# Down projection of a two-layer decoder trunk: seven block products for eight of its eleven K pairs, in two passes of 512 channels

## The chip, the cores and the metric

The kernel runs on one core of a Trainium2 chip. The metric is the device time of one execution in microseconds (us); smaller is better. Engines are named as in the profile: PE is TensorE (PEld its weight loads), DVE VectorE, ACT ScalarE, POOL GpSimd, SP SyncE, which issues most transfers.

## What is computed

Two layers, each with four mixers side by side, an output projection and a SwiGLU block. The change is in the last but two lines:

```python
x = x + rms_norm(y, attn_post_g[l])
h = rms_norm(x, ffn_pre_g[l])
f = jax.nn.silu(jnp.einsum('bsd,df->bsf', h, w_gate[l])) * jnp.einsum('bsd,df->bsf', h, w_up[l])
f = jnp.einsum('bsf,fd->bsd', f, w_down[l])
x = x + rms_norm(f, ffn_post_g[l])
```

Here s is 512 tokens, d is 1024, and the hidden width f is 2816, which is 22 blocks of 128. All is float32; the result of one layer is the x of the next.

## The kernel before

Each float32 operand of a large product is held as two float16 parts, hi and lo, and every product is three matmuls (hi hi, hi lo, lo hi; `split3`, line 582). Weights come from memory as "slots" of 128 x 2048 float32 (1 MB), in four parts of 512 columns, into the buffer `raw`, which holds two slots and four more parts. For each part ACT copies raw to the hi half of a place in the float16 buffer `ring` (`split_hi_chunk`, recorded at line 925), and DVE writes the lo half (`split_lo_part`, line 1413). `ring` has 32 "quads" of 1024 float16 each: an ordinary slot takes four, a fast one seven. ACT and DVE are strictly in program order; a split waits on them until the quads it overwrites are free, and SP loads the next part of raw when DVE has read the old one.

PE walks a list `UNITS` of (slot, token tiles). Per layer: ten slots of the input projection, four of the output projection, 22 of gate/up (one for each hidden block f) and eleven of the down projection (each has two K blocks of 128, the "pair"). Between the matmuls of a unit PE places small products (attention, transposes) at numbered ticks; the table `AT` says which tick, and `h_T` (eight transposes of a normalised tile) is entered there as `pre_T` and `fpre_T`.

**Gate/up.** The hidden blocks 5 to 21 (`FAST`) are already made by seven products of 256 columns instead of eight (`seven_products`, line 661): 84 matmuls per block. Their weight sums are made by two DVE additions (lines 1389, 1392) and two adding transfers from POOL. Within a unit PE waits for ACT and DVE four times: `p1_copied` (ACT copies the first product), `u_sb` and `v_sb` (ACT copies of sums, `u_copy`, `v_copy`) and `c12_ps` (a DVE addition, `c12_add`, line 1450). Beside the unit of block f, `main_steps` of ACT and DVE also finish the hidden block f-1 (`silu` line 1100, `hidden` line 1780, `hidden_hi`, `hidden_lo` line 1788) and split the weights that follow, in four chunks between these steps. At the end of gate/up two slots of the down projection are split beside one unit, because they need only four quads each.

**Down.** For each slot and tile PE makes 12 matmuls of 512 columns, 24 for a pair and 512 channels over all four tiles. The four results of the tiles lie in the eight PSUM banks (`pair(t)`). The first seven slots run over all tiles; of the last four (`DN_TAIL`) all are done for tile 0, then tile 1, 2 and 3, so that the norm of a finished tile runs beside the next ones: per tile ACT squares (`square_y`), DVE makes the root (seven instructions, `rstd`) and adds to x (`norm_y`, lines 1492 and 1495), ACT squares x, DVE makes the root and `norm_x` (line 1527), PE transposes (`h_T`), ACT and DVE write `hT` (`h_hi_of`, `h_lo_of` line 1535). In the last layer `norm_out` (lines 1508, 1511) takes the place of `norm_y` and the tile is stored.

```python
split_lo(*REST[l])
norm_y("fpost", l, 0)
norm_x("pre", l + 1, 0)
norm_y("fpost", l, 1)
```

`REST[l]` are the slots whose split follows after gate/up: in layer 0 the last down slots 44 to 46 and the first four of layer 1 (47 to 50).

## Time and profile before

| | us |
|---|---|
| median of 3 runs (1065.86 to 1069.61) | 1068.95 |
| the profiled execution, its own time | 1068.87 |
| its span in the trace | 1067.1 |
| PE busy | 1044.1 (98%) |
| DVE busy | 759.4 (71%) |
| ACT busy | 498.6 (47%) |
| share of the chain that ended last: PE / DVE / ACT | 92% / 3% / 2% |

Times of the trace count from the start of the span. A busy PE is not a PE at its peak, since matmuls overlap and their ends are modelled; the distance between the starts of matmuls is what counts.

### The profile page before, as it was taken

The page shows a single profiled execution, that of the slowest core. Times are in us where ns is not written, and L with a number is a line of the kernel's source. Part 1 is how long each engine was busy: PE and PEld are TensorE (multiplying, and loading weights), DVE is VectorE, ACT ScalarE, POOL GpSimd, SP SyncE. Part 2 cuts the span into 40 slices and gives each one's busy share as a digit, 9 for nine tenths or more (in the row PEclk, how much of TensorE's full clock was granted, in tenths as well). Part 3 has the DMA queues.
Part 4 walks back from the last instruction along what each step waited for, and adds up shares of the span by engine and source line. Part 5 has one row for each costly group of instructions (what it writes and reads, how often), then busy time and mean ns, then how long its engine had stood idle before and what let it go on. Part 6 is the DMA issues. An engine that isn't in the chain of part 4 may idle for free.

```text
span 1067.1 us, 19775 instructions
## 1 busy us (share of the span) xinstructions
PE 1044.1 (98%) x7894; PEld 776.7 (73%) x7894; DVE 759.4 (71%) x1571; ACT 498.6 (47%) x928; POOL 65.2 (6%) x86
## 2 busy tenths in 40 slices
PE   7999999999999999999999999999999999999997
PEld 5988895597888887444488888747878888864443
DVE  6999988987777877222679888898867777661014
...
DMA packets 72876, 136.59 MB, mean 128 GB/s; under 512 B 8657, under 2 KB 8913, under 8 KB 72657
## 3 DMA queue, kind: packets, MB, share of 16 engines
...
## 4 chain that ended last, share of the span: by engine, by line
PE 92%; DVE 3%; ACT 2%; issue 1%; DMA 1%; SPq 0%; ACTq 0%; DVEq 0%
PE ps L589 56%; PE ps L696 28%; PE ps L593 3%; PE ps L855 1%; PE ps L839 1%; DVE ring L1413 1%; ACT ring L925 1%; DMA xs<-x_dram 1%; PE ps L774 1%; PE ps L759 0%; DVE E L1527 0%; ACT gbc L925 0%; PE ps L816 0%; PE ps L777 0%; DVE hT L1535 0%
## 5 line engine op out<-in xcount | busy, mean ns | idle before, releaser
L1413 DVE SCALAR_TENSOR_TENSOR ring<-raw,ring 128x512 f16<-128x512 f32 (+1 forms) x368 | 293.4, 834 | 142.7 <-ACT ring L925 142.7
L925 ACT ACTIVATE ring<-raw 128x512 f16<-128x512 f32 (+1 forms) x368 | 252.0, 741 | 139.9 <-PE ps L589 76.7
L589 PE MATMUL ps<-ring,U 128*128 128x512 f16 x1440 | 313.4, 379 | 0.0
L589 PEld LDWEIGHTS ps<-ring,U 128*128 128x128 f16 x1440 | 140.8, 98 | 166.7 <-issue 0.3
L589 PE MATMUL ps<-hT,ring 128*128 128x256 f16 (+1 forms) x1632 | 195.2, 279 | 0.0
L589 PEld LDWEIGHTS ps<-hT,ring 128*128 128x128 f16 x1632 | 159.3, 98 | 28.9
L696 PE MATMUL ps<-E,ring 128*128 128x256 f16 x1224 | 146.7, 274 | 5.7 <-ACT ps L925 5.7
L696 PE MATMUL ps<-hT,ring 128*128 128x256 f16 x1224 | 146.1, 273 | 0.0
L589 PE MATMUL ps<-ring,hT 128*128 128x256 f16 x1152 | 134.8, 275 | 0.7 <-DVE hT L1535 0.7
L696 PEld LDWEIGHTS ps<-E,ring 128*128 128x128 f16 x1224 | 118.2, 98 | 22.9 <-ACT ps L925 7.4
L696 PEld LDWEIGHTS ps<-hT,ring 128*128 128x128 f16 x1224 | 120.2, 98 | 14.4
L589 PEld LDWEIGHTS ps<-ring,hT 128*128 128x128 f16 x1152 | 113.0, 99 | 15.8 <-issue 1.1
L1575 DVE SCALAR_TENSOR_TENSOR E<-E,par 128x256 f32<-128x256 f32 x240 | 102.1, 481 | 0.2
L566 POOL DMA_DIRECT2D raw<-weights_dram x34 | 29.8, 876 | 810.1 <-DMA raw<-weights_dram 810.1
L1100 ACT ACTIVATE R<-ps 128x512 f32<-128x512 f32 (+1 forms) x52 | 27.5, 528 | 92.4 <-PE ps L696 72.7
L1463 DVE TENSOR_SCALAR small<-small 128x1 f32<-128x1 f32 x31 | 4.6, 150 | 85.8 <-ACT E L935 77.2
L935 ACT ACTIVATE E<-ps 128x1024 bf16<-128x1024 f32 x15 | 15.3, 1019 | 90.6 <-PE ps L589 90.6
L696 PE MATMUL ps<-Z,ring 128*128 128x256 f16 x408 | 50.1, 273 | 0.0
L925 ACT ACTIVATE U<-ps 128x256 f32<-128x256 f32 (+3 forms) x56 | 30.2, 565 | 42.1 <-PE ps L593 15.3
L696 PEld LDWEIGHTS ps<-Z,ring 128*128 128x128 f16 x408 | 39.9, 98 | 4.6
L1780 DVE SCALAR_TENSOR_TENSOR R<-ps,R 128x512 f32<-128x512 f32 (+1 forms) x52 | 31.4, 604 | 5.8 <-ACT R L1100 5.1
L925 ACT ACTIVATE gbc<-ps 128x128 f32<-128x128 f32 (+3 forms) x32 | 13.9, 434 | 45.5 <-PE ps L855 36.2
...
## 6 DMA issues: line engine op xcount, KB each, us to landing
raw<-weights_dram SPq DMA_DIRECT2D x402, 256.0 KB, 3.5
raw<-weights_dram POOLq DMA_DIRECT2D x68, 256.0 KB, 6.1
...
U<-weights_dram SPq DMA_DIRECT2D x8, 256.0 KB, 7.7
out_dram<-xs SPq DMA_DIRECT2D x8, 256.0 KB, 2.0
...
bd<-pool_w_dram SPq DMA_DIRECT2D x8, 16.0 KB, 9.5
```

The costliest lines, as they stand in the source:

```text
L566: nc.gpsimd.dma_start(raw[:, x1, :], weights[PARTS * n, :, :], accum_op=ALU.add).then_inc(x1_sum[i % 2], 16)
L589: ins = mm(dst, st, mv_, start=first and i == 0, stop=last and i == 2, **kw)
L593: return nc.tensor.transpose(dst, src, ident)
L696: ins = mm(bank[b][:, 0:HALF], quad(n, q, pw)[:, cols], a[pa][:, k, :], start=first and k == 0 and j == 0, stop=last and k == KT // 2 - 1 ...
L774: last = mm(o[:, h, :], sm[:, h, :], rv[:, t, HD * h:HD * (h + 1)], start=h == 0, stop=t == 0 and h == NH - 1, skip_group_check=True)
L839: mm(bank[b][:, 0:P * (t + 1)], mqT[r, t % 2, h // 2, :], mkT[r, h // 2, 0:P * (t + 1)], start=False, stop=True, skip_group_check=True).th ...
L925: return A(dst, src, ACT.Copy, scale=scale)
L935: A(sink[:, :], pair(t), ACT.Square, scale=UNSCALE * DM ** -0.5, accum_out=ssq[:, t:t + 1]).then_inc(y_sq, 1)
L1100: A(like_gu(f, sil[:, n % 2, 0:P * len(tiles)]), gu_tiles(f, tiles)[0], ACT.Silu, scale=UNSCALE).then_inc(sil_done, 1)
L1413: V.scalar_tensor_tensor(out=at[1], in0=src, scalar=W_SCALE, in1=at[0], op0=ALU.mult, op1=ALU.subtract).then_inc(lo_split, 1)
L1575: ins = V.scalar_tensor_tensor(out=cacc[:, c, :], in0=src, scalar=w, in1=cacc[:, c, :], op0=ALU.mult, op1=ALU.add)
L1780: V.scalar_tensor_tensor(out=like_gu(f, fbuf[:, n % 2, 0:w]), in0=gu_tiles(f, tiles)[1], scalar=UNSCALE * A_SCALE * (-1.0 if f in FAST els ...
```

## The change

The pairs 2 to 9 of hidden blocks (blocks 4 to 19, `DN_FAST`) are multiplied as 2 x 2 blocks with seven products instead of eight: K is halved into the two blocks of a pair, tokens into halves of 256, and channels into quarters of 256. The channels are taken in two passes g of 512, so an item is (g, pair); it has 42 matmuls of 256 columns (`dn_seven`). The pairs 0, 1 and 10 (`PLAIN`) stay as they were; pair 10 follows the seven-product items of each pass, and pairs 0 and 1 are left for the end, tile by tile.

- The four sums of the hidden activations of a pair are made in gate/up, beside the unit after the pair's odd block: three DVE instructions (`fS_sums`), two ACT copies (`fS_hi`), two DVE instructions (`fS_lo`).
- The weight sums of an item are made by three DVE instructions (`dn_weight_sums`) before its split, which has 768 and 1024 columns instead of 512 and 512.
- After a pass the seven running sums in PSUM are combined: two ACT copies (`q11_copy`), six DVE instructions (`q_sums`); in pass 0 four more that add the pair-10 result (`y0_sums`). The combined sums lie in SBUF, and each finished tile gets them by one more DVE addition (`y_sum`) before its norm.
- Nine of the 32 quads now hold the activation sums of six pairs during gate/up and down (two pairs' lie in `Z` and `E`), so gate/up and down have 23. Only one slot is split beside a gate/up unit.
- ACT makes `p1_copy` after the first chunk of the split instead of the second.
- The transposes of tiles 0 and 1 for the next layer move: tile 0 to nine ticks before the end, tile 1 from layer 0 to tick 4 of layer 1, tiles 2 and 3 to ticks 26 and 52.
- The tail of the down projection has 30 matmuls of 512 columns for each tile (before: 48).

```diff
--- before.py
+++ after.py
-DN_TAIL = 4
 FAST = tuple(range(GU_HEAD + 1, FT))
+DN_FAST = tuple(range(2, 10))
+PLAIN = tuple(p for p in range(N_DN) if p not in DN_FAST)
+COVER = PLAIN[-1]
+ITEMS = [(0, p) for p in DN_FAST] + [(0, COVER)] + [(1, p) for p in DN_FAST] + [(1, COVER)]
+ITEMS += [(g, p) for p in PLAIN[:-1] for g in range(2)]
...
-UNITS += [(DN0, (t,)) for t in (2, 3, 0, 1)]
-UNITS += [(DN0 + c, (t,)) for c in range(1, N_DN - DN_TAIL) for t in TILES]
-UNITS += [(DN0 + c, (t,)) for t in TILES for c in range(N_DN - DN_TAIL, N_DN)]
+COVER_TILES = (2, 3, 0, 1)
+TAIL0 = 2 * len(DN_FAST) + 1
+WORK = {}
+
+
+def add_dn_unit(tiles, items):
+    WORK[len(UNITS)] = items
+    UNITS.append((DN0 + items[0] // 2, tiles))
+
+
+for k in range(TAIL0):
+    if ITEMS[k][1] == COVER:
+        for t in COVER_TILES:
+            add_dn_unit((t,), (k,))
+    else:
+        add_dn_unit(TILES, (k,))
+for t in TILES:
+    add_dn_unit((t,), (TAIL0,))
+    for k in range(TAIL0 + 1, len(ITEMS), 2):
+        add_dn_unit((t,), (k + 1, k))
...
+GU_RING = 23
...
+    if slot >= DN0:
+        size = (sum(HALF_QUADS[n]) + 1) // 2
+        top = top if top + size <= GU_RING else 0
+        places = list(range(top, top + size))
...
-        ("fpre_T", 0): 372, ("fpre_T", 1): 374, ("fpre_T", 2): 415, ("fpre_T", 3): 438, ("pre_T", 0): 955,
-        ("pre_T", 1): 965,
+        ("fpre_T", 0): 372, ("fpre_T", 1): 374, ("fpre_T", 2): 415, ("fpre_T", 3): 438, ("pre_T", 0): TICKS - 9,
...
-        ("pre_T", 2): 0, ("pre_T", 3): 31, ("moba_T", 0): 65, ("moba_T", 1): 82, ("moba_stage", 0): 106,
+        ("pre_T", 1): 4, ("pre_T", 2): 26, ("pre_T", 3): 52, ("moba_T", 0): 65, ("moba_T", 1): 82, ("moba_stage", 0): 106,
...
+                products = (
+                    (3, s1, [PAIR[3]], [(q_sb, q0 + 6)]),
+                    (4, s3, [PAIR[2]], [(q_sb, q0 + 3)]),
+                    (6, a22, [PAIR[2] + 1, PAIR[3] + 1], y_free[2:4]),
+                    (0, a11, [PAIR[0]], [(q11_sb, 2 * (2 * l + g) + 2)]),
+                    (5, s2, [PAIR[1]], [(q_sb, q0 + 2)]),
+                    (2, a12, [PAIR[0] + 1, PAIR[1] + 1], y_free[0:2]),
+                    (1, s4, [PAIR[0] + 1, PAIR[1] + 1], None))
+                for i, (blk, a, banks, free) in enumerate(products):
+                    if i:
+                        between(i)
+                    if first and free:
+                        for b, f_ in zip(banks, free):
+                            take(b, *f_)
+                    for t in range(2):
+                        if len(banks) == 1:
+                            dst, fresh = bank[banks[0]][:, HALF * t:HALF * (t + 1)], t == 0
+                        else:
+                            dst, fresh = bank[banks[t]][:, half(int(blk == 1))], blk != 1
+                        for c, (pw, pa) in enumerate(((0, 0), (1, 0), (0, 1))):
+                            ins = mm(dst, a[pa][:, tok(t)], dn_blocks(n, j, pw, blk, blk + 1),
+                                     start=first and fresh and c == 0, stop=last_ and c == 2, skip_group_check=True)
+                return ins
...
+            def fS_hi(l, p):
+
+                act.wait_ge(s_sum, 3 * fS_no(l, p))
+                copy(fS_w[p][:, 0, :], f_sum[:, 0:3 * HALF]).then_inc(s_hi, 1)
+                copy(fT[:, 0, 2 * p, half(1)], f_sum[:, 3 * HALF:4 * HALF]).then_inc(s_hi, 1)
...
-                    split_hi_chunks(new, 0, 2)
+                    split_hi_chunks(new, 0, 1)
                     if f in FAST:
                         p1_copy(l, f)
-                    split_hi_chunks(new, 2, 3)
+                    split_hi_chunks(new, 1, 3)
                     hidden_hi(l, *HIDDEN[i - 1])
                     if f in FAST:
                         u_copy(l, f)
+                    fp = HIDDEN[i - 1][0]
+                    if fp % 2 and in_seven(fp):
+                        fS_hi(l, fp // 2)
                     split_hi_chunks(new, 3, 4)
                     if f in FAST:
...
+                V.tensor_tensor(dn_sum(j)[:, 0:2 * HALF].rearrange("p (c t) -> p c t", c=2),
+                                three[:, 0:2 * HALF].rearrange("p (c t) -> p c t", c=2),
+                                b12.unsqueeze(1).to_broadcast([P, 2, HALF]), ALU.add).then_inc(x_sum, 1)
+                dve.wait_ge(x_sum, at + 1)
+                V.tensor_tensor(x[2], x[0], b22, ALU.add).then_inc(x_sum, 1)
+                dve.wait_ge(x_sum, at + 2)
+                V.tensor_tensor(x[3], x[2], b21, ALU.add).then_inc(x_sum, 1)
...
+                V.tensor_tensor(f_sum[:, 0:2 * HALF].rearrange("p (c t) -> p c t", c=2),
+                                f_all[:, HALF:3 * HALF].rearrange("p (c t) -> p c t", c=2),
+                                f_all[:, 3 * HALF:4 * HALF].unsqueeze(1).to_broadcast([P, 2, HALF]),
+                                ALU.subtract).then_inc(s_sum, 1)
+                dve.wait_ge(s_sum, i + 1)
+                V.scalar_tensor_tensor(out=f_sum[:, 2 * HALF:3 * HALF], in0=f_sum[:, 0:HALF], scalar=-1.0,
+                                       in1=f_all[:, 2 * HALF:3 * HALF], op0=ALU.mult,
+                                       op1=ALU.subtract).then_inc(s_sum, 1)
+                dve.wait_ge(s_sum, i + 2)
+                V.tensor_tensor(f_sum[:, 3 * HALF:4 * HALF], f_sum[:, 2 * HALF:3 * HALF], f_all[:, 0:HALF],
+                                ALU.add).then_inc(s_sum, 1)
...
+            def fS_lo(l, p):
+
+                dve.wait_ge(s_hi, 2 * fS_no(l, p))
+                V.tensor_tensor(fS_w[p][:, 1, :], f_sum[:, 0:3 * HALF], fS_w[p][:, 0, :],
+                                ALU.subtract).then_inc(s_lo, 1)
+                V.tensor_tensor(fT[:, 1, 2 * p, half(1)], f_sum[:, 3 * HALF:4 * HALF], fT[:, 0, 2 * p, half(1)],
+                                ALU.subtract).then_inc(s_lo, 1)
...
+            def q_sums(l, g):
...
+                for t in range(2):
+                    V.tensor_tensor(yq[2 + t][:, 512 + HALF:DM], p6[:, half(t)], yq[t][:, 512:512 + HALF],
+                                    ALU.add).then_inc(q_sb, 1)
+                dve.wait_ge(q_sb, i + 2)
+                V.tensor_tensor(yq23[:, :, 512:512 + HALF], p7[:, :].rearrange("p (t c) -> p t c", t=2),
+                                yq23[:, :, 512 + HALF:DM], ALU.add).then_inc(q_sb, 1)
+                for t in range(2):
+                    V.scalar_tensor_tensor(out=yq[t][:, 512 + HALF:DM], in0=p5[:, half(t)], scalar=-1.0,
+                                           in1=yq[2 + t][:, 512 + HALF:DM], op0=ALU.mult,
+                                           op1=ALU.subtract).then_inc(q_sb, 1)
+                dve.wait_ge(q_sb, i + 5)
+                V.scalar_tensor_tensor(out=yq23[:, :, 512 + HALF:DM], in0=p5[:, :].rearrange("p (t c) -> p t c", t=2),
+                                       scalar=-1.0, in1=yq23[:, :, 512:512 + HALF], op0=ALU.mult,
+                                       op1=ALU.subtract).then_inc(q_sb, 1)
+
+            def y0_sums(l):
...
+                for t in COVER_TILES:
+                    dve.wait_ge(unit_done, l * NU + COVERED[t] + 1)
+                    V.tensor_tensor(yq[t][:, 0:512], bank[PAIR[t] + 1][:, :], yq[t][:, 512:DM],
+                                    ALU.add).then_inc(y0_sb, 1)
...
+                    V.tensor_tensor(pair(t), pair(t), yq[t], ALU.add).then_inc(y_add, 1)
...
+                    due = fp % 2 and in_seven(fp)
+                    if due:
+                        fS_sums(l, fp // 2)
                     if f in FAST:
                         c12_add(l, f)
                     split_lo_chunks(new, 2, 3)
                     if f in FAST:
                         c22_add(l, f)
+                    if due:
+                        fS_lo(l, fp // 2)
                     split_lo_chunks(new, 3, 4)
                 hidden(l, *HIDDEN[i1 - 1])
...
-                split_lo(*REST[l])
+                sums_due = 0
+                for n in REST[l]:
+                    if sums_due < 2 and FREE_AFTER[n] > l * NU + LAST_SEVEN[sums_due]:
+                        q_sums(l, sums_due)
+                        if sums_due == 0:
+                            y0_sums(l)
+                        sums_due += 1
+                    split_lo(n)
+                for g in range(sums_due, 2):
+                    q_sums(l, g)
+                    if g == 0:
+                        y0_sums(l)
+                y_sum(l, 0)
                 norm_y("fpost", l, 0)
                 norm_x("pre", l + 1, 0)
+                y_sum(l, 1)
                 norm_y("fpost", l, 1)
                 norm_x("pre", l + 1, 1)
+                h_lo_of("pre", l + 1, 0)
+                y_sum(l, 2)
                 norm_y("fpost", l, 2)
-                h_lo_of("pre", l + 1, 0)
                 h_lo_of("pre", l + 1, 1)
+            y_sum(L - 1, NT - 1)
```

What moves in the order. First DVE in gate/up, beside the unit that follows a pair's odd block, from the hidden block's lo half (`R` hidden, `U` its float16 home) to the last chunk of the split. Before:

```order
L1788 TENSOR_TENSOR U<-R,U 128x512 [waits f_hi]
L1450 TENSOR_TENSOR ps<-ps,gt 128x256 [waits u_sb]
L1392 TENSOR_TENSOR raw<-raw 128x512 [waits x_sum,raw_in3]
L1413 SCALAR_TENSOR_TENSOR ring<-raw,ring 128x2x512 [waits hi_split]
L1456 TENSOR_TENSOR ps<-ps,gt 128x256 [waits v_sb]
L1413 SCALAR_TENSOR_TENSOR ring<-raw,ring 128x2x512 [waits hi_split]
```

After:

```order
L2031 TENSOR_TENSOR U<-R,U 128x512 [waits f_hi]
L2040 TENSOR_TENSOR gbc<-R 128x512 [waits s_lo,f_sb]
L2045 SCALAR_TENSOR_TENSOR gbc<-gbc,R 128x256 [waits s_sum]
L2049 TENSOR_TENSOR gbc<-gbc,R 128x256 [waits s_sum]
L1690 TENSOR_TENSOR ps<-ps,gt 128x256 [waits u_sb]
L1605 TENSOR_TENSOR raw<-raw 128x512 [waits x_sum,raw_in7]
L1653 SCALAR_TENSOR_TENSOR ring<-raw,ring 128x2x512 [waits hi_split]
L1696 TENSOR_TENSOR ps<-ps,gt 128x256 [waits v_sb]
L2055 TENSOR_TENSOR ring<-gbc,ring 128x768 [waits s_hi]
L2057 TENSOR_TENSOR U<-gbc,U 128x256
L1653 SCALAR_TENSOR_TENSOR ring<-raw,ring 128x2x512 [waits hi_split]
```

Three additions stand ahead of the one PE waits for (L1450, now L1690), and two more instructions after `c22_add` (L1456, now L1696). Then ACT beside the same unit, from `silu` on. Before:

```order
L1100 ACTIVATE R<-ps 128x512 [waits f_sb,unit_done]
L925 ACTIVATE ring<-raw 128x512 [waits raw_in4,unit_done]
L925 ACTIVATE ring<-raw 128x2x512 [waits raw_in7,raw_in6]
L925 ACTIVATE ps<-ps 128x256 [waits p1_ps]
L925 ACTIVATE ring<-raw 128x2x512 [waits x2_sum0,x1_sum0]
L925 ACTIVATE U<-R 128x512 [waits f_sb]
L925 ACTIVATE gt<-ps 128x256 [waits c12_ps,p6_ps]
L925 ACTIVATE ring<-raw 128x2x512 [waits x_sum]
L925 ACTIVATE gt<-ps 128x256 [waits c22_ps,p7_ps]
```

After:

```order
L1275 ACTIVATE R<-ps 128x512 [waits f_sb,unit_done]
L1097 ACTIVATE ring<-raw 128x512 [waits raw_in0,unit_done]
L1097 ACTIVATE ps<-ps 128x256 [waits p1_ps]
L1097 ACTIVATE ring<-raw 128x2x512 [waits raw_in3,raw_in2]
L1097 ACTIVATE ring<-raw 128x2x512 [waits x2_sum1,x1_sum1]
L1097 ACTIVATE U<-R 128x512 [waits f_sb]
L1097 ACTIVATE gt<-ps 128x256 [waits c12_ps,p6_ps]
L1097 ACTIVATE ring<-gbc 128x768 [waits s_sum]
L1097 ACTIVATE U<-gbc 128x256
L1097 ACTIVATE ring<-raw 128x2x512 [waits x_sum]
L1097 ACTIVATE gt<-ps 128x256 [waits c22_ps,p7_ps]
```

The copy of the first product (`ps<-ps`) comes one chunk earlier; two copies of activation sums (`fS_hi`) stand ahead of the last chunk and of `v_copy`, the last row. Third, DVE at the end of layer 0: its last splits and the norm of tile 0. Before:

```order
L1413 SCALAR_TENSOR_TENSOR ring<-raw,ring 128x512 x28
L1463 TENSOR_SCALAR small<-small 128x1
L1467 TENSOR_SCALAR small<-small 128x1
L1469 TENSOR_SCALAR small<-small 128x1
L1471 SCALAR_TENSOR_TENSOR small<-small 128x1
L1473 SCALAR_TENSOR_TENSOR small<-small 128x1
L1475 TENSOR_SCALAR small<-small 128x1
L1477 SCALAR_TENSOR_TENSOR small<-small 128x1
L1492 SCALAR_TENSOR_TENSOR ps<-ps,small,gbc 128x1024
L1495 SCALAR_TENSOR_TENSOR xs<-ps,xs 128x1024
```

After (`R`, `E`, `Z` on the left hold the combined sums of the tiles):

```order
L2069 TENSOR_TENSOR R<-ps,E 128x256 [waits y0_sb,q11_sb,unit_done]
L2069 TENSOR_TENSOR R<-ps,Z 128x256
L2072 TENSOR_TENSOR R<-ps,R 128x2x256 [waits q_sb]
L2075 SCALAR_TENSOR_TENSOR E<-ps,R 128x256
L2075 SCALAR_TENSOR_TENSOR Z<-ps,R 128x256
L2079 SCALAR_TENSOR_TENSOR R<-ps,R 128x2x256 [waits q_sb]
L1653 SCALAR_TENSOR_TENSOR ring<-raw,ring 128x512 [waits hi_split] x16
L2098 TENSOR_TENSOR ps<-ps,E 128x1024 [waits unit_done,q_sb]
L1703 TENSOR_SCALAR small<-small 128x1 [waits y_sq]
```

The splits of slots 47 to 50 (the 16) now stand behind the combination of pass 1, which waits for the last seven-product unit, and ahead of tile 0's added sum.

## Rows read from the trace of the kernel before

**Rows 1.** The page, busy time of the engines over the span
```profile
PE 1044.1 (98%) x7894; PEld 776.7 (73%) x7894; DVE 759.4 (71%) x1571; ACT 498.6 (47%) x928; POOL 65.2 (6%) x86
```
**Rows 2.** The chain that ended last: start us, us, what
```profile
263.01 9.17 PE ps L696 x84
272.40 119.22 PE ps L696 x1092
...
521.26 0.87 PE ps L593 x8
...
782.65 9.17 PE ps L696 x84
...
945.39 113.97 PE ps L589 x528
```
**Rows 3.** Waits of PE: for whom, us in total, times, longest us
```profile
PE ps L696 <- ACT ps L925: 5.7, 6, 3.6
```
**Rows 4.** Stages: us, busy (instructions) of PE, PEld, DVE, ACT, POOL, PEclk, DMA, GB/s
```profile
908.00:912.00 4.00, 3.69 (x19) 2.65 (x20) 2.71 (x5) 3.04 (x7) 0.00 (x0) 0.58 0.61 197
```
**Rows 5.** Timeline of ACT beside one gate/up unit: start us, us, instruction [idle before]
```profile
299.95 0.60 ACT L1100 ACTIVATE R<-ps 128x512 f32<-128x512 f32 x1 [2.09 <-PE ps L696]
300.44 1.57 ACT L925 ACTIVATE ring<-raw 128x512 f16<-128x512 f32 x2
301.91 0.37 ACT L925 ACTIVATE ps<-ps 128x256 f32<-128x256 f32 x1
...
303.16 0.62 ACT L925 ACTIVATE U<-R 128x512 f16<-128x512 f32 x1
...
305.70 1.06 ACT L925 ACTIVATE ring<-raw 128x1024 f16<-128x1024 f32 x1 [1.43 <-DVE raw L1392]
306.66 0.36 ACT L925 ACTIVATE gt<-ps 128x256 f32<-128x256 f32 x1
```
**Rows 6.** Timeline of DVE beside the same unit
```profile
304.05 0.68 DVE L1788 TENSOR_TENSOR U<-R,U 128x512 f16<-128x512 f32 x1
304.65 0.43 DVE L1450 TENSOR_TENSOR ps<-ps,gt 128x256 f32<-128x256 f32 x1
304.98 0.68 DVE L1392 TENSOR_TENSOR raw<-raw 128x512 f32<-128x512 f32 x1
305.58 1.22 DVE L1413 SCALAR_TENSOR_TENSOR ring<-raw,ring 128x1024 f16<-128x1024 f32 x1
```
**Rows 7.** Timeline of PE: the sixth of the seven products of the same unit
```profile
306.30 1.47 PE L696 MATMUL ps<-Z,ring 128*128 128x256 f16 x12
```
**Rows 8.** Timeline at the end of layer 0: last split, norm of tile 0
```profile
494.12 2.50 DVE L1413 SCALAR_TENSOR_TENSOR ring<-raw,ring 128x512 f16<-128x512 f32 x4 [7.86 <-ACT ring L925]
503.81 1.02 ACT L935 ACTIVATE E<-ps 128x1024 bf16<-128x1024 f32 x1 [8.17 <-PE ps L589]
...
506.54 1.29 DVE L1492 SCALAR_TENSOR_TENSOR ps<-ps,small,gbc 128x1024 f32<-128x1024 f32 x1
507.87 1.22 DVE L1495 SCALAR_TENSOR_TENSOR xs<-ps,xs 128x1024 f32<-128x1024 f32 x1
...
511.88 1.28 DVE L1527 SCALAR_TENSOR_TENSOR E<-xs,small,gbc 128x1024 f32<-128x1024 f32 x1
```
**Rows 9.** The page, DMA issues: KB each, median us from issue to landing
```profile
raw<-weights_dram SPq DMA_DIRECT2D x402, 256.0 KB, 3.5
```
**Rows 10.** Timeline of the last layer's tile 0: its square, last write of its output
```profile
1028.31 1.02 ACT L935 ACTIVATE E<-ps 128x1024 bf16<-128x1024 f32 x1 [49.61 <-PE ps L589]
...
1033.22 0.69 DVE L1511 SCALAR_TENSOR_TENSOR xs<-ps,xs 128x512 f32<-128x512 f32 x1
```
**Rows 11.** Timeline at the start of layer 1: two lo halves of `hT`, end of `moba_rotate`, `moba_T`
```profile
548.32 2.50 DVE L1535 SCALAR_TENSOR_TENSOR hT<-ps,hT 128x1024 f16<-128x1024 f32 x2
...
554.65 0.29 DVE L1627 TENSOR_TENSOR U<-E 128x128 f32<-128x128 f32 x1
...
559.48 0.60 PE L593 MATMUL ps<-cst,U 128*128 128x128 f32 x4
```

301 lines of the change are left out of this document (243 added, 58 removed).

## The prediction

> **What bounds the kernel now.** I read the page first: PE is busy for 1044.1 of the span's 1067.1 us [rows 1], so the time is what PE executes plus its few stops. The chain of waits gives the price of its work: 1092 matmuls of 256 columns in 119.22 us are 0.1092 us each, 528 of 512 columns (one layer's down projection) in 113.97 us are 0.2158 us each, eight transposes 0.87 us [rows 2]. The waits of PE show that ACT's copies stopped it six times for 5.7 us, once for 3.6 us [rows 3]; after that one the granted clock was 0.58 on average over 4 us [rows 4], so part of them at 1.2 GHz. The timelines of ACT and DVE beside one gate/up unit [rows 5 to 7] show how near their work is to PE's waits, and the one at the layer's end [rows 8] what stands between a finished tile and the next layer.
>
> **1. Matmuls of the down projection.** Eight pairs by two passes are 16 items of 42 matmuls per layer: 672 x 0.1092 = 73.4 us. The three plain pairs keep 144 of 512 columns: 31.1 us. Together 104.5 instead of 114.0, a gain of 9.5 us per layer, **19.0 us**. The 256-column price comes from the same alternation of weight load and matmul, with weight loads hidden [rows 2].
> The Trainium skill (TensorE: Matmul & The Clock Gate, section Back-to-back issue gap) gives a sustained 131 ns for 512 columns and 81 ns for 128; read on a straight line that is some 98 ns for 256, and by this estimate an item would take 4.1 instead of 3.1 us and the change would cost 31 us. The rows contradict the 131 ns with 215.8, so the sum goes by the rows.
>
> **2. Gate/up, stops that go.** Seventeen fast units of 84 matmuls need 17 x 9.17 = 155.9 us. Three times a layer the last units have two slots' splits beside one, and PE stops there because ACT makes `p1_copy` only after half of them. The six stops are 5.7 us [rows 3]; with the slow matmuls after the longest (0.42 of 4 us, 1.7 us [rows 4]) and the drained pipeline around each they are **8.2 us** in all: the fast stretch of layer 1, from 782.65 to 945.39, is 6.8 us longer than 155.9 [rows 2], and layer 0's three stops of 0.4 us and the refilling of the pipeline add 1.4. Only one slot is split beside a unit now, and `p1_copy` stands earlier, so all of it goes; the lower bound is 5.7.
>
> **3. Gate/up, stops that come.** Take t = 0 at the start of a unit; the sixth product starts at 5 x 1.31 = 6.56, which puts it at 299.75 [rows 7]. In the trace `hidden_lo` starts at 4.30, `c12_add` ends at 5.33, DVE's second weight sum at 5.91, ACT's last chunk runs from 5.95 to 7.01 and `v_copy` ends at 7.27 [rows 5, 6]; PE wants `c12` at 6.56 and `v_sb` at 7.87. Slack: 1.2 and 0.6 us. Beside the unit after a pair's odd block the change puts three DVE instructions before `c12_add`: 512 columns 0.68, and two of 256, for which I take the 0.43 of the addition in PSUM [rows 6]; each waits for the one before, about 0.04. They fill 4.94 to 6.55, `c12_add` ends at 6.89, and PE goes on at 6.94 instead of 6.56. The weight sum ends at 7.48. ACT meanwhile makes `fS_hi` of 768 columns (0.83, between the 0.62 for 512 and 1.06 for 1024 [rows 5]) and 256 (0.37) from 6.58 to 7.68, then the last chunk to 8.64, and `v_copy` ends at 8.91. PE's seventh product starts at 8.96 instead of 7.87: **1.1 us** per such unit. `fS_lo` (0.95 + 0.43) and the last chunk end at 11.7, 1.4 us into the next unit, where DVE idled until 1.35 before; that unit has no sums and half a `hidden_lo` (0.43 for 0.68), so nothing is passed on. Of the eight such units seven also split a fast slot; the last of them splits none and costs nothing. With 0.3 us where the first down slot is split beside block 21: 8.0 per layer, **16.0 us**. Ends: 0 (if the new instructions are as short as to fit the slack), and 2 x 8 x 2.9 = 46 if all DVE work of a pair (0.68 + 0.86 + 1.38) lay on the path. I take the schedule, which is nearest to the rows.
>
> **4. Inside the down projection** nothing is late: an item's weight sums take 1.6 us (0.68 + 2 x 0.43 and the waits), its two lo halves 0.95 and 1.22 with 0.1 of waiting for ACT, 3.9 us against 4.59 for PE. The splits left from gate/up end 1.4 us after pass 0; `q_sums` takes 2.9 more, 4.3 against the 5.2 us of pair 10 that cover it. Its margin is 0.9 us, and without that cover it costs up to 4.
>
> **5. Between the layers.** Let T be the end of the last seven-product unit of layer 0. PE then has 120 matmuls of 512 columns (25.9), four `h_T` (3.5) and 195 matmuls of 256 columns (21.3) before layer 1's first `moba_T`: T + 50.7. Before, DVE had ended its splits at 496.6, 7.2 us before ACT began on tile 0 [rows 8], and PE had no stop: the chain has only its transposes and matmuls there [rows 2]. Now `q_sums` ends at T + 3.9 (two ACT copies 1.0, six instructions 2.9) and the splits of slots 47 to 50 follow, 2.5 us each [rows 8], of which the last two also wait for transfers of 3.5 us [rows 9] into parts that DVE frees only then: T + 13.4. Tile 0 was done at T + 6.5. Its chain is `y_sum` 1.2, then what took from 503.81 to 513.16 in the trace, 9.35 [rows 8], and a wait of 0.1: `norm_x` ends at T + 24.1. PE wants it at T + 20.1: a stop of 4.0. Tile 1 stands behind it on DVE: T + 34.7, and only then `h_lo` of tile 0 (1.2 [rows 11]): T + 35.9, for which PE waits again, having ended the layer at T + 31 or, at half clock, 33. `h_lo` of tile 1 stands behind tile 2's sum and norm (1.2 + 1.15 + 1.6 + 2.55, then its own 1.2): T + 43.6; third stop. Then `norm_x` of tile 2 (T + 46.5), tile 3 (10.6: T + 57.1), the split of slot 51 (2.5), `h_lo` of tiles 2 and 3 (T + 62.3), one more split and `moba_rotate` (1.8): T + 66.5, where `moba_T` can start. Before, DVE was there 4.5 us ahead of PE [rows 11]. **15.8 us** are lost. Half clock after the stops lies in time that PE waits anyway. Ends: 4.0 (only tile 0 is late) and 20.3 (if the 4.5 us of lead is also missed later).
>
> **6. The end.** `norm_out` takes 5.6 us from square to last write [rows 10]; with `y_sum` and the step between engines 6.9, while PE makes a tile in 6.5. DVE reaches tile 3 some 1.4 us after PE's end, and adds two halves of 0.68 before ACT's square: **2.7 us** (bounds 0.7 and 4).
>
> **Sum** against the profiled execution's 1068.87 (span 1067.1, 1.8 around it; the median of the runs is 1068.95, the same within 0.1): -19.0 - 8.2 + 16.0 + 15.8 + 2.7 = +7.3, **1076.2 us**. 0.5%, 5.3 us, is about what a measurement of this kernel can tell from no change.
>
> **The rivals.** (a) One large stop is absent: either DVE's sums slip into the slack of gate/up, or the transition costs 4 instead of 15.8. For it: DVE is busy for 71% only [rows 1]. Against: it is in program order, and the rows show the slack as 0.6 and 1.2 us. 1076.2 - 16 or - 11.8: 1060 to 1064. (b) Both are absent: 1076.2 - 27.8 = 1048. (c) Both are about half as long, since transfers, the order of ACT's copies or a shorter 256-column instruction help: 8 + 6 us less give 1062, less help up to 1070. (d) DVE's delay runs on: layer 1's attention goes by it, and PE stops at each small product until DVE has regained its lead. It decides once DVE reaches layer 1 more than 4.5 us late, which by part 5 it does; price 4.5 to 7, and 4 more if `q_sums` of pass 0 loses its cover: up to 1087, slower by 18. (e) The change doesn't make the down projection shorter: 256-column matmuls with new stationary data each time cost 0.123 us, which is 42 x 0.123 = 24 x 0.2158. Then 1076.2 + 19 = 1095. Against: 1092 of them at 0.1092.
> The skill's sustained rates (the section named above) would give the sign of (e); by [rows 2] the trace does not agree.
>
> **How the numbers follow.** My schedule as it stands, 1071 to 1081: 0.45. (a) 0.17. (b) 0.05. (c) 0.14, of which a quarter lies below 1063.5. (d) 0.15. (e) 0.04. The range takes the first, (a) down to its lower part, (c) and (d): 1058 to 1087. Faster than 1063.5: (b), two thirds of (a), that quarter: 0.20. Slower than 1074.3: 0.36 of the first, (d) and (e): 0.55. The rest, 0.25, within 0.5%.
>
> **What would show it.** In the profile after: each layer's 672 matmuls at 0.109 us; in gate/up PE stops before the sixth and seventh product beside blocks 6, 8 ... 18, about 0.4 and 0.7 us, and none at `p1_copied`; DVE's lo halves of slots 47 to 50 after `q_sums`; three stops of 2 to 5 us around the layer boundary released by `norm_x` and `h_lo`; the last matmul some 10.4 us before the end instead of 7.7. Wrong would be a gate/up of 156 us, a boundary where PE doesn't stop for DVE, or seven-product items much longer than 4.6 us.

## The result, and the profile after

| | before | after |
|---|---|---|
| median, us | 1068.51 (4 runs, 1065.86 to 1069.61) | 1079.92 (4 runs, 1077.32 to 1081.74) |
| profiled execution, its own time / span | 1068.87 / 1067.1 | 1077.32 / 1075.5 |

The ratio is 1.0109 with a 95% interval of 1.0079 to 1.0138: slower by 1.1%. The prediction was 1076.2, and the profiled execution is 1.1 us above it; the median lies 3.7 us above it, inside the range. Two figures have to be kept apart below: the trace shows the fastest of the four executions (mean granted clock 0.996; the others 0.989 to 0.991).

The page of the changed kernel, busy times (compare [rows 1]); transfers still take 3.5 us ([rows 9]):
```profile
PE 1029.6 (96%) x8470; PEld 831.2 (77%) x8470; DVE 897.9 (83%) x1788; ACT 540.0 (50%) x968; POOL 65.1 (6%) x86
```
PE is busy for 14.5 us less and the span is 8.4 us longer, so it idles 23 us more. DVE has 139 us more. The waits of PE say where (for whom, us in total, times, longest):
```profile
PE ps L704 <- DVE E L1767: 8.5, 4, 4.5
PE ps L700 <- DVE hT L1775: 8.1, 4, 3.8
PE ps L808 <- ACT gt L1097: 8.0, 14, 0.6
PE ps L808 <- DVE ps L1690: 3.3, 14, 0.2
...
PE ps L704 <- DVE U L1867: 2.2, 1, 2.2
...
PE ps L877 <- DVE R L2079: 1.2, 2, 0.6
```
The old wait [rows 3] for `p1_copy` is gone. `ACT gt` and `DVE ps` are `v_copy` and `c12_add`, fourteen times each, seven per layer. `E`, `hT` and `U` are `norm_x`, `h_lo` and `moba_rotate`: 13.7 of their 18.8 us lie around the layer boundary; the rest lies elsewhere, and the kernel before had as much of it (5.1). `R L2079` is `q_sums`.

The chain that ended last (start, us, what) gives the stages; compare [rows 2]:
```profile
262.29 9.17 PE ps L808 x84
...
469.18 36.86 PE ps L877 x336
...
795.87 9.17 PE ps L808 x84
...
1002.79 36.85 PE ps L877 x336
```
The first fast block starts at 262.29 (before 263.01), layer 1's at 795.87 (782.65). With the first down matmuls, at 426.73 and 960.32 in the chain's reckoning (before 420.90 and 945.39; PE's timeline has the same starts 0.16 earlier), the span divides into five stretches:

| stretch | before | after | difference |
|---|---|---|---|
| to layer 0's first fast block | 263.0 | 262.3 | -0.7 |
| layer 0, fast blocks | 157.9 | 164.4 | +6.5 |
| layer 0 down, to layer 1's first fast block | 361.8 | 369.1 | +7.4 |
| layer 1, fast blocks | 162.7 | 164.4 | +1.7 |
| layer 1 down and end | 121.7 | 115.2 | -6.5 |

**Inside the down projection**, PE's timeline at the first product of pass 1, and DVE's at the same place:
```profile
463.25 5.34 PE L898 MATMUL ps<-ring,U 128*128 128x512 f16 x24
469.18 1.47 PE L877 MATMUL ps<-ring,Z 128*128 128x256 f16 x12 [0.58 <-DVE R L2079]
```
```profile
462.30 0.69 DVE L1617 TENSOR_TENSOR raw<-raw 128x512 f32<-128x512 f32 x1
463.03 0.42 DVE L1621 TENSOR_TENSOR raw<-raw 128x256 f32<-128x256 f32 x1
463.49 0.42 DVE L1623 TENSOR_TENSOR raw<-raw 128x256 f32<-128x256 f32 x1
463.83 0.95 DVE L1653 SCALAR_TENSOR_TENSOR ring<-raw,ring 128x768 f16<-128x768 f32 x1
465.03 1.22 DVE L1653 SCALAR_TENSOR_TENSOR ring<-raw,ring 128x1024 f16<-128x1024 f32 x1 [0.25 <-ACT ring L1097]
466.18 0.42 DVE L2069 TENSOR_TENSOR R<-ps,E 128x256 f32<-128x256 f32 x1
...
468.34 0.69 DVE L2079 SCALAR_TENSOR_TENSOR R<-ps,R 128x512 f32<-128x512 f32 x1
```
Eight seven-product items fill 426.57 to 463.25, 36.68 us, which is 336 x 0.1092 (to 0.01). DVE's item is 0.7 + 0.45 + 0.4 for the weight sums, 0.95 and 1.22 for the halves, 0.25 idle between them because ACT's copy runs beside the first half, and 0.1 to the next item: 4.1 us, not 3.9. That is still less than PE's 4.59, so DVE doesn't fall behind item by item. But it has nine seven-product items and one plain one to split ahead of `q_sums` (slots 37 to 41, the last three items already of pass 1), and it works on them without waiting for PE from 428.0 to 466.2: 2.9 us after the pass (466.18 against 463.3) instead of 1.4. So the last `q_sums` ends at 469.0, and PE stopped for 0.6 us in each layer.

**Beside one gate/up unit**, the one after a pair's odd block, in the timelines of PE and DVE (before: [rows 6, 7], where PE has no stop and nothing stands ahead of `c12_add`):
```profile
336.94 1.48 PE L808 MATMUL ps<-Z,ring 128*128 128x256 f16 x12 [0.23 <-DVE ps L1690]
338.99 2.79 PE L808 MATMUL ps<-hT,ring 128*128 128x256 f16 x24 [0.57 <-ACT gt L1097]
```
```profile
334.94 0.68 DVE L2040 TENSOR_TENSOR gbc<-R 128x512 f32<-128x512 f32 x1
335.65 0.43 DVE L2045 SCALAR_TENSOR_TENSOR gbc<-gbc,R 128x256 f32<-128x256 f32 x1
336.11 0.42 DVE L2049 TENSOR_TENSOR gbc<-gbc,R 128x256 f32<-128x256 f32 x1
336.45 0.42 DVE L1690 TENSOR_TENSOR ps<-ps,gt 128x256 f32<-128x256 f32 x1
```
Two stops, 0.23 for `c12_add` (336.45, behind the three sums of 334.94 to 336.45) and 0.57 for `v_copy`. With the empty pipeline behind each, two units take 19.50 us (the second stop's row comes again at 358.49 in the chain) instead of 18.34: 1.15 us per pair, where the prediction had 1.1.

**Around the layer boundary** (before: [rows 8, 11]). The last seven-product unit ends at T = 505.9. PE's timeline:
```profile
530.59 1.74 PE L704 MATMUL ps<-cst,E 128*128 128x128 f32 x8 [4.49 <-DVE E L1767]
...
542.35 1.47 PE L700 MATMUL ps<-ring,hT 128*128 128x256 f16 x12 [3.15 <-DVE hT L1775]
...
549.83 6.07 PE L700 MATMUL ps<-ring,hT 128*128 128x256 f16 x54 [3.83 <-DVE hT L1775]
...
572.65 0.66 PE L704 MATMUL ps<-cst,U 128*128 128x128 f32 x4 [2.24 <-DVE U L1867]
```
and DVE, last splits, then its steps up to the second rotation:
```profile
509.60 10.41 DVE L1653 SCALAR_TENSOR_TENSOR ring<-raw,ring 128x512 f16<-128x512 f32 x16
519.93 1.22 DVE L2098 TENSOR_TENSOR ps<-ps,E 128x1024 f32<-128x1024 f32 x1
...
529.25 1.28 DVE L1767 SCALAR_TENSOR_TENSOR E<-xs,small,gbc 128x1024 f32<-128x1024 f32 x1
...
539.78 1.28 DVE L1767 SCALAR_TENSOR_TENSOR E<-xs,small,gbc 128x1024 f32<-128x1024 f32 x1
...
548.56 1.21 DVE L1775 SCALAR_TENSOR_TENSOR hT<-ps,hT 128x1024 f16<-128x1024 f32 x1
...
561.96 1.28 DVE L1767 SCALAR_TENSOR_TENSOR E<-xs,small,gbc 128x1024 f32<-128x1024 f32 x1
...
572.31 0.29 DVE L1867 TENSOR_TENSOR U<-E 128x128 f32<-128x128 f32 x1
```
Four stops, 13.7 us. DVE is at each step within 0.7 us of where the prediction put it: `q_sums` T + 3.7 (3.9), splits T + 14.0 (13.4), `norm_x` of tiles 0, 1, 3 T + 24.6, 35.1, 57.3 (24.1, 34.7, 57.1), `h_lo` of tile 1 T + 43.9 (43.6), `moba_rotate` T + 66.7 (66.5).

The end, PE's last group of matmuls:
```profile
1059.55 5.99 PE L898 MATMUL ps<-ring,U 128*128 128x512 f16 x27
```
It ends at 1065.5, 10.0 us before the end of the span.

From the first `moba_T` to layer 1's first fast block PE takes 223.1 us (572.65 to 795.71 in its timeline); before it took 223.0 (559.48, [rows 11], to 782.48). Behind the boundary nothing more is lost.

### The profile page after: what moved, and what is told of

Its sections match the earlier page's. It is cut to its first block, busy times and chain, and to the rows that moved or that the text cites. A ratio compares the mean times of both kernels' runs of the same rounds, so it can differ in the third digit from the quotient of the medians.

```text
span 1075.5 us, 21327 instructions
## 1 busy us (share of the span) xinstructions
PE 1029.6 (96%) x8470; PEld 831.2 (77%) x8470; DVE 897.9 (83%) x1788; ACT 540.0 (50%) x968; POOL 65.1 (6%) x86
## 4 chain that ended last, share of the span: by engine, by line
PE 64%; DVE 20%; ACT 9%; issue 5%; DMA 2%; SPq 1%; DVEq 0%; ACTq 0%
PE ps L700 31%; PE ps L808 18%; PE ps L877 7%; ACT ring L1097 6%; DVE ring L1653 5%; PE ps L704 3%; DMA raw<-weights_dram 1%; PE ps L1029 1%; DVE raw L1617 1%; PE ps L1013 1%; DVE R L2022 1%; DVE gbc L2040 1%; DVE raw L1623 1%; DVE raw L1621 1%; DVE ps L2098 1%
## 5 line engine op out<-in xcount | busy, mean ns | idle before, releaser
L1653 DVE SCALAR_TENSOR_TENSOR ring<-raw,ring 128x512 f16<-128x512 f32 (+2 forms) x368 | 320.6, 902 | 70.6 <-ACT ring L1097 70.3
L1097 ACT ACTIVATE ring<-raw 128x512 f16<-128x512 f32 (+2 forms) x368 | 275.1, 796 | 135.6 <-DVE raw L1623 71.8
L877 PE MATMUL ps<-ring,U 128*128 128x256 f16 x768 | 94.3, 273 | 0.0
L700 PE MATMUL ps<-ring,U 128*128 128x512 f16 x384 | 84.9, 379 | 0.0
L898 PE MATMUL ps<-ring,U 128*128 128x512 f16 x288 | 64.0, 383 | 0.0
L877 PE MATMUL ps<-ring 128*128 128x256 f16 x432 | 55.0, 273 | 0.0
```

Of the source, the lines that this page charges most:

```text
L700: ins = mm(dst, st, mv_, start=first and i == 0, stop=last and i == 2, **kw)
L877: ins = mm(dst, a[pa][:, tok(t)], dn_blocks(n, j, pw, blk, blk + 1), start=first and fresh and c == 0, stop=last_ and c == 2, skip_group_c ...
L898: ins = mm(bank[b][:, :], fT[:, pa, f, tok(t)], dn_quad(n, j, c, pw), start=fresh and c == 0 and i == 0, stop=c == 1 and i == 2, skip_grou ...
L1097: return A(dst, src, ACT.Copy, scale=scale)
L1653: V.scalar_tensor_tensor(out=at[1], in0=src, scalar=W_SCALE, in1=at[0], op0=ALU.mult, op1=ALU.subtract).then_inc(lo_split, 1)
```

## The experiments

Every one is compared with the kernel before on the same chip. The differences to the changed kernel are differences of medians; of that kernel there are two, 1079.92 and 1080.71.

**1. Gate/up: the sums behind PE's two waits.** In `main_steps` of DVE and ACT:
```diff
-                    if due:
-                        fS_sums(l, fp // 2)
                     if f in FAST:
                         c12_add(l, f)
                     split_lo_chunks(new, 2, 3)
                     if f in FAST:
                         c22_add(l, f)
                     if due:
-                        fS_lo(l, fp // 2)
+                        fS_sums(l, fp // 2)
                     split_lo_chunks(new, 3, 4)
+                    if due:
+                        fS_lo(l, fp // 2)
...
-                    if fp % 2 and in_seven(fp):
-                        fS_hi(l, fp // 2)
                     split_hi_chunks(new, 3, 4)
                     if f in FAST:
                         v_copy(l, f)
+                    if fp % 2 and in_seven(fp):
+                        fS_hi(l, fp // 2)
```


> Edit: in gate/up the sums of a pair's activations (three DVE instructions) stand behind c12_add, the next chunk and c22_add instead of ahead of c12_add; fS_hi stands behind v_copy on ACT and fS_lo behind the last chunk on DVE. The work is the same. Theory A (the stops are a matter of the order on DVE and ACT): both stops beside a pair's unit go, two units take 18.34 instead of 19.49 us, a layer's gate/up about 156.5 instead of 164.3; the time is 1079.9 - 16 = 1064 (1062 to 1067). Rival B (DVE has too much to do there, 2.9 us more per pair): the stops come back a unit later, at c12 or at the silu of the next block, and the time stays at 1076 to 1081.

Measured: 1075.95, 4.0 less; ratio to before 1.0065 (1.0052 to 1.0078). PE's timeline has one stop of 0.20 per pair and two new large ones, for `u_copy` and `v_copy`:
```profile
326.09 2.79 PE L808 MATMUL ps<-hT,ring 128*128 128x256 f16 x24 [0.20 <-ACT gt L1097]
...
418.21 1.48 PE L808 MATMUL ps<-E,ring 128*128 128x256 f16 x12 [1.18 <-ACT gt L1097]
...
422.01 1.49 PE L808 MATMUL ps<-hT,ring 128*128 128x256 f16 x12 [1.01 <-ACT gt L1097]
```
The seven pairs gave some 0.75 us each per layer, 5.2; the stops of 1.18 and 1.01, both in block 21's unit (not 20 and 21, as the expectation of experiment 6 has it), took 2.4 of it back, where `fS_lo` and the first down slot's weight sums now stand one after the other on DVE. From the first fast block to pass 1 a layer takes 204.0 us instead of 206.9, so 5.8 for both, and the median fell by 4.0 and 4.8 against the two of the changed kernel. The time is at the edge of B's range (1076 to 1081) and far from A's (1062 to 1067). A named the mechanism and not its size: some 0.4 us per pair stayed, and work moved out of the way of one wait came to stand in front of others, as B said, though only beside block 21.

**2. The boundary: only another order.** Slots 47 to 50 behind `norm_x` of tile 0, on both engines:
```diff
                 norm_x("pre", l + 1, 0)
+                if l + 1 < L:
+                    split_lo(*range((l + 1) * SLOTS, (l + 1) * SLOTS + 4))
                 y_sum(l, 1)
```


> Edit: the splits of slots 47 to 50 (layer 1's first four) stand behind norm_x of tile 0 instead of ahead of y_sum of tile 0, on ACT and DVE alike. Theory A (what counts between the layers is the sum of DVE's work and waits up to moba_rotate, 66.7 us after the last seven-product unit): the stop of 4.5 us at the first transpose goes, and the later ones grow by as much; moba_T starts within 1.5 us of where it did; 1079.9, within 1078 to 1081.5. Rival D (each stop is a loss of its own, to be removed by itself): 1079.9 - 4.5 = 1075.4, or less.

Measured: 1082.03, ratio 1.0126 (1.0112 to 1.0140), 1.3 and 2.1 above the two medians of the changed kernel; a little over what theory A allowed, and far from D. PE's waits:
```profile
546.26 2.72 PE L700 MATMUL ps<-ring,hT 128*128 128x256 f16 x12 [13.13 <-DVE hT L1777]
...
576.57 0.85 PE L704 MATMUL ps<-cst,U 128*128 128x128 f32 x4 [2.24 <-DVE U L1869]
```
The stop at the first transpose is gone and the next one is 13.13 us. D fell: a stop removed by this order came back at the next step, since DVE's sum of work and waits up to `moba_rotate` is what PE waits for. That sum even grew, against the first profile by more than A's 1.5 us: `moba_T` starts 70.4 us after the last seven-product unit, where the changed kernel has 66.8 and, in the second profile (5), 69.3. DVE now reaches tile 0 before PE has finished it and waits 2.93 us there.

**3. The boundary: the splits in DVE's idle gaps.** While ACT squares, DVE idles for 1.2 us, twice per tile:
```diff
                 y_sum(l, 0)
+                next_lo(l, 4, 6)
                 norm_y("fpost", l, 0)
+                next_lo(l, 6, 8)
                 norm_x("pre", l + 1, 0)
```
and so on for tiles 1 to 3 (parts 8 to 15, and `h_lo` of tiles 0 and 1 in gaps too), with ACT's copies in the same order. A second thing moves as well: slots 51 and 52, which stood ahead of `moba_rotate`, are split behind it.
```diff
-                split_lo(z + 4)
+                if l == 0:
+                    split_lo(z + 4)
                 h_lo_of("pre", l, 2)
                 h_lo_of("pre", l, 3)
-                split_lo(z + 5)
+                if l == 0:
+                    split_lo(z + 5)
                 moba_rotate(l, 0)
+                if l:
+                    split_lo(z + 4, z + 5)
```

> Edit: slot 47 is still split right behind the last q_sums, but the twelve parts of slots 48 to 50 stand two by two in the gaps where DVE waits for ACT's square within the norms of tiles 0 to 3; h_lo of tiles 0 and 1 stand in such gaps too, and slots 51 and 52 behind moba_rotate. The work is the same. Theory A (DVE's work from the last seven-product unit to moba_rotate sets layer 1's start, and its idle gaps of 1.2 us, eight in all, are what can be won): moba_T starts about 56 instead of 66.8 us after that unit, and the time is 1079.9 - 11 = 1069 (1067 to 1072). Rival F (the chain of square, root and norm over ACT and DVE, 10.5 us a tile, sets it and not the splits; or the transfers that the later splits release come too late for PE): 1075 to 1081.

Measured: 1074.86, ratio 1.0059 (1.0045 to 1.0073), 5.1 to 5.9 less. PE:
```profile
538.14 6.07 PE L700 MATMUL ps<-ring,hT 128*128 128x256 f16 x54 [1.97 <-DVE hT L1797]
...
561.96 0.65 PE L704 MATMUL ps<-cst,U 128*128 128x128 f32 x4
...
572.60 1.08 PE L704 MATMUL ps<-cst,U 128*128 128x128 f32 x4 [4.42 <-ACT U L1097]
```
`moba_T` of tile 0 starts at 561.96, 56.2 us after the last seven-product unit, as theory A said, and without a wait; 10.6 us were won there. DVE's timeline up to the end of `moba_rotate` divides them (us):

| DVE | splits | other work | idle |
|---|---|---|---|
| changed kernel | 15.0 (24 parts) | 41.8 | 9.9 |
| experiment 3 | 9.6 (16 parts) | 41.9 | 4.7 |

Idle gaps gave 5.2; the other 5.4 are the eight parts of slots 51 and 52, which only moved behind the point that PE waits for. Neither half was run alone.

Two stops of 2.04 and 0.91 for `norm_x` remain, and `moba_T` of tile 1 now waits 4.42 us for an ACT copy queued behind the splits of slots 51 to 54; on the way ACT stood 2.25 + 0.54 us for transfers of slot 53. So 4.4 of the 10.6 us came back 11 us later, in the way of the part of theory F that speaks of transfers. The time lies between A's range (1067 to 1072) and F's (1075 to 1081).

**4. The old stops, alone.** In the kernel before:
```diff
-                    split_hi_chunks(new, 0, 2)
+                    split_hi_chunks(new, 0, 1)
                     if f in FAST:
                         p1_copy(l, f)
-                    split_hi_chunks(new, 2, 3)
+                    split_hi_chunks(new, 1, 3)
```


> Edit: the kernel before, with ACT's p1_copy behind the first quarter of a unit's chunks instead of behind the first half (the one line of the change that bears on the old stops). Theory A (half of my 8.2 us term or more is that line): the stops of 5.7 us and the slow matmuls behind the long one go, 1068.5 - 8.2 = 1060.3; by the stops alone 1062.8. Rival G (with two slots' splits beside one unit ACT is late with another copy instead, u or v, so that only the change's new places of the splits remove the stops): 1066 to 1069.

Measured: 1064.79, ratio 0.9959 (0.9947 to 0.9971), 4.2 less than before. The five short stops are gone, the long one is only shorter and has another releaser:
```profile
908.09 2.74 PE L696 MATMUL ps<-E,ring 128*128 128x256 f16 x12 [2.54 <-ACT gt L925]
```
So the line by itself is worth half of my 8.2 us. Rival G's range (1066 to 1069) was missed, but its mechanism holds in one of the six places where two slots are split beside a unit, which had the long stop: beside block 18 of layer 1 one of the two is a fast slot (82), and ACT stands 1.51 us for its weight sum before it comes to its copy. At the other five, with two down slots, the line was enough. In the changed kernel neither stop is left.

**5. The changed kernel once more**, as a base.

> The changed kernel unaltered, as the common base of this group. All theories: 1079.9 us, 1077 to 1082. Theory H (part of what the profiled execution, 1077.3, does not show is the clock after the four stops between the layers): a second profile of the same program lists the same stops within 0.1 us, and any difference of its span lies in stretches behind these stops with a granted clock below 1.

Measured: 1080.71 (4 runs, 1079.23 to 1082.05), ratio 1.0121 (1.0106 to 1.0137); the profiled execution has a span of 1080.3, 4.8 more than the first one. The stops are the same to 0.3 us but for the first (5.32 for 4.49) and a last one before gate/up (1.55 at 763.68 for 0.58 at 758.98). The matmuls behind the third and fourth are not (those behind the first are slow in both, with a granted clock of 0.74 and 0.72 from 528 to 534). The second profile's PE timeline (the first's rows are above, 549.83 and 572.65):
```profile
550.24 7.74 PE L700 MATMUL ps<-ring,hT 128*128 128x256 f16 x54 [3.84 <-DVE hT L1775]
...
575.47 7.14 PE L700 MATMUL ps<-ring,hT 128*128 128x256 f16 x51
```
and two stages of each profile, the first's and then the second's (us, busy of PE, PEld, DVE, ACT, POOL, granted clock, DMA share, GB/s):
```profile
550.00:554.00 4.00, 4.00 (x39) 3.58 (x38) 3.61 (x9) 0.11 (x1) 0.00 (x0) 1.00 0.01 2
...
576.00:580.00 4.00, 4.00 (x39) 3.63 (x37) 4.00 (x11) 0.59 (x2) 0.00 (x0) 1.00 0.46 142
```
```profile
550.00:554.00 4.00, 3.76 (x22) 2.82 (x23) 3.67 (x10) 0.23 (x2) 0.00 (x0) 0.63 0.01 4
...
576.00:580.00 4.00, 4.00 (x28) 3.09 (x27) 3.96 (x10) 1.61 (x4) 0.00 (x0) 0.70 0.78 224
```
Behind the third stop (3.83 and 3.84 us) 54 matmuls took 6.07 us in the first profile and 7.74 in the second, with a granted clock of 0.63 from 550 to 554, so partly at 1.2 GHz. Behind the fourth, 51 matmuls took 5.73 and 7.14 (0.70 from 576 to 580). From pass 1 of layer 0 to layer 1's first fast block the second profile is 5.1 us longer: 1.7 and 1.4 are these matmuls, 0.8 and 1.0 the two longer stops. H stands for the larger part. Its other half, equal stops within 0.1 us, fell, and ACT's timeline shows why. Ahead of the first stop, while slots 47 to 50 are split, ACT waited 4.2 us for transfers instead of 3.1. Ahead of the last one it waited 5.72 us for one (up to 757.41) instead of 2.94 (up to 750.89).

**6. Gate/up, second form**: as 1, but `fS_lo` one unit later, behind that unit's `c22_add`.
```diff
-                    if due:
-                        fS_lo(l, fp // 2)
+                    if i > i0 and fp % 2 == 0 and in_seven(fp - 1):
+                        fS_lo(l, fp // 2 - 1)
```


> Edit: as the first gate/up experiment (sums behind c22_add, fS_hi behind v_copy), but fS_lo stands one unit later, behind that unit's c22_add, where DVE was seen idle for 1.1 us. Theory A' (the first form only passed 1.3 us of fS_lo on to the next unit and to the last two blocks, which are near to their limit): the 0.2 us stop per pair and the stops of 1.2 and 1.0 us beside blocks 20 and 21 go; two units take 18.35 us, a layer's fast stretch 156 to 157; 1079.9 - 15 = 1065 (1063 to 1070, since up to 5 of it can be lost to transfers and to the clock between the layers, as in the first form). Rival B (DVE has no room for 2.9 us more per pair): stops of over 0.2 us per pair remain, 1072 to 1077.

Measured: 1069.38 (12 runs), ratio 1.0016 (1.0006 to 1.0026), 11.3 less than the base of its group. PE's waits:
```profile
PE ps L877 <- DVE R L2079: 2.0, 2, 1.0
PE ps L808 <- ACT gt L1097: 1.7, 2, 0.9
```
The 28 stops are gone, and one of 0.85 per layer, beside block 21, is new. Two units take 18.55 us, 0.2 more than 168 x 0.1092, without a wait that the trace lists. A' holds, near the slow end of its range. Of the 16.2 us that the stops beside the pairs cost (14 x 1.16), 14 x 0.2 stayed, the two new stops with the pipeline behind them took 2.0, and `q_sums` of pass 0, which ended 0.5 later in each layer, 1.0: 10.4 by this count, 11.3 by the medians. B fell: DVE had room for the work, but not in that place.

**7. The boundary, second form**: as 3, and in layer 1 `m_T_copy(l, 0)` ahead of `split_hi(z + 6)` instead of behind `split_hi(z + 7)`.

> Edit: as the experiment that put splits into the gaps of the norms, and in layer 1 ACT makes m_T_copy of tile 0 ahead of the splits of slots 53 and 54 instead of behind them. Theory A'' (the 10.6 us won at moba_T of tile 0 were cut by one stop of 4.4 us at moba_T of tile 1, where ACT stood in front of a transfer with that copy queued behind it): that stop goes or falls below 1 us and the time is 1074.9 - 4 = 1071 (1069 to 1072.5). Rival J (PE stops at the next thing, a slot that is split late, by as much): 1074 to 1076.

Measured: 1074.81, ratio 1.0068 (1.0056 to 1.0080): nothing gained over 3 (1074.86). The stop went, and another came:
```profile
584.93 0.48 PE L704 MATMUL ps<-cst,gbc 128*128 128x128 f32 x1 [3.56 <-ACT gbc L1249]
```
It waits for ACT's exponent (line 1249), which waits for the row maximum `m_max` on DVE. A'' fell and J's range holds the time, though the next thing was not a split slot but DVE's queue.

**8. Both second forms.**

> Edit: the two of this group together. Theory A: the two terms are in different places and add: 1079.9 - 15 - 9 = 1056 (1054 to 1061), faster than the kernel before by 0.7 to 1.4%. Rival K (what gate/up gives back is lost again between the layers, since DVE and the transfers set layer 1's start whatever comes before): layer 0's half is lost, 1063 to 1066.

Measured: 1063.71 (6 runs), ratio 0.9965 (0.9952 to 0.9979): 17.0 below the changed kernel, and 11.3 + 5.9 = 17.2 is what the two gave apart. The terms add. The time is above the 1054 to 1061 expected and inside K's range (1063 to 1066), but K was priced with parts that each gave less than their stops: had half of gate/up's 11.3 been lost again, the time would be 1069. Some of what K describes is there all the same. In the profiles PE needs 2.6 us more from layer 0's first down matmul to layer 1's fast blocks than in experiment 7 (369.1 for 366.5), and the stop for the exponent is longer:
```profile
PE ps L704 <- ACT gbc L1249: 5.0, 1, 5.0
```

**9. And `m_max` earlier**: in layer 1
```diff
-                conv(l, 0, 18)
+                if l == 0:
+                    conv(l, 0, 18)
                 m_max(l, 0, 0)
-                conv(l, 0, 1)
+                conv(l, 0, 10 if l else 1)
                 m_max(l, 0, 1)
-                conv(l, 0, 1)
+                conv(l, 0, 10 if l else 1)
```


> Edit: as the experiment with both parts together, and in layer 1 DVE makes the first m_max (of moba stage 0) ahead of the second group of 18 + 2 taps of conv instead of behind 18 of them. Theory L (the fill moved DVE's backlog, not removed it: the stop of 5.0 us at 581 is PE waiting for an exponent behind m_max, which stands behind 7.2 us of conv while its input was there at 572): that stop goes, 1063.7 - 5 = 1059 (1058 to 1061). Rival M (DVE's backlog is what counts, and conv, 7 us later than before at its reader, stops PE instead by as much): 1062 to 1065.

Measured: 1061.46 (5 runs, 1060.42 to 1061.63), ratio 0.9933 (0.9919 to 0.9946), 2.3 less than 8 (3.4 by the two ratios to the kernel before), between L's range (1058 to 1061) and M's (1062 to 1065). It beats the kernel before by 0.7%, and by 3.3 us the kernel before with one line changed (4; medians of two groups). The first exponent no longer stops PE, but the second and third do, 3.9 us for 5.0, each behind ten taps of `conv` that now follow the `m_max` before it:
```profile
577.33 0.23 PE L1010 MATMUL ps<-cst 128*128 128x128 bf16 x1 [1.48 <-ACT gbc L1249]
...
583.30 0.63 PE L704 MATMUL ps<-cst,U 128*128 128x128 f32 x4 [2.44 <-ACT gbc L1249]
```
So the order brought part of the stop's 5.0 us, as L said, and DVE's backlog kept the rest, as M said.

## Why the prediction was right, and where it was off

**Part 1 (-19.0)** held: 672 matmuls per layer at 0.1092 us, the price of [rows 2]. Rival (e) fell by the same numbers. The sustained 131 ns that the Trainium skill gives (TensorE: Matmul & The Clock Gate, section "Back-to-back issue gap"), weighed there, stays contradicted: the chain after has 336 matmuls of 256 columns in 36.86 us, where the straight line to 131 ns gave some 98 ns each. Another section of the same page of the Trainium skill, "Wait — 56ns, not 53.3ns?", gives a start-to-start distance of N / 2.4 GHz plus about 2.5 ns when warm. For 256 columns that is, as an estimate, 109.2 ns, and the trace agrees (36.68 us for 336).

**Parts 2 and 3 (-8.2 + 16.0 = +7.8)** held: the fast blocks grew by 6.5 and 1.7, 8.2 in all. Layer 0 of experiment 4, with no stop, takes 156.1 us for them; against it the old stops were 8.4 and the new ones 16.7. Per pair 1.15 us for 1.1, and its two stops stand where the schedule put them. The three sums took 0.68, 0.43 and 0.42. The Trainium skill (VectorE: DVE Perf Modes, section "The TRN2 errata — SBUF-src ops pay a fixed extra latency per instruction") gives (N + 151) / 0.96 ns for a float32 addition, 0.691 us for 512 columns and, as an estimate by the same formula, 0.424 for 256; the trace agrees to 0.01. Experiment 6 shows that the places of this work on DVE and ACT are the cause: with the same work behind the waits 11.3 us go. Experiment 4 divides part 2: the place of `p1_copy` by itself is worth 4.2, and the long stop, which part 2 put down to that place like the short ones, mostly stays, because a fast slot and a down slot are split beside that unit.

**Part 4 ("nothing is late")** is the step that failed. It took 3.9 us for DVE's item by adding durations, with 0.1 of waiting for ACT where 0.25 is idle and nothing for the step to the next item, and let the splits ahead of `q_sums` end 1.4 us after the pass. Nine such items stand there; 0.2 more for each is 1.8 us, and they ended 2.9 us after it. The margin of 0.9 us is gone, and PE stops for 0.6 twice, 1.5 us with the pipeline behind them.

**Part 5 (+15.8)** held as a schedule. "Layer 0 down, to layer 1's first fast block" is +7.4, which is -9.5, +0.75 for `q_sums` and so 16.1 for the boundary. Experiment 2 shows that it is the sum of DVE's queue, waits included, and not its first stop. Experiment 3 shows 10.6 us of that sum to be avoidable: 5.2 of idle gaps, and 5.4 of splits that `moba_rotate` need not wait for. One sentence of it failed: "Half clock after the stops lies in time that PE waits anyway". It holds behind the first stop, where the next wait follows. Behind the third it made the transpose of tile 3 late, for which DVE's last `h_lo` waited 2.12 us instead of 0.47; behind the fourth no wait follows. That is 1.7 and 1.4 us in the second profile. The first profile, with a mean clock of 0.996, did not pay them; the seven other executions of the two groups have 0.989 to 0.992 and are 1.6 to 4.7 us longer. Among the seven the clock doesn't order the times (1079.23 has 0.989, 1082.05 has 0.992), and 1.8 us of the second profile's 5.1 come from longer waits for transfers. Part 4's 1.5 us, which the first profile contains, and these two together are of the size of the median's 3.7 us above the forecast. How often each stop lets the clock fall, and what the other executions paid, was not measured.

**Part 6 (+2.7)**: the last matmul ends 10.0 us before the end, for 10.4; +2.3.

Of the rivals, (a), (b) and (c) are excluded by the 28 stops in gate/up and the four at the boundary. (d), that DVE's delay runs on into attention, was not seen in the changed kernel: from `moba_T` to the fast blocks PE takes 223.1 us for 223.0, and the wait ahead of layer 1's gate/up, 0.58 us, was 0.60 before (1.55 in the second profile). Its mechanism was seen in experiments 7 to 9, where the boundary was compressed, and DVE's queue became the bound at the first exponents. What limits a still better version there is open: whether 9's last two stops can go without a wait elsewhere wasn't tried.
